# A two-layer trunk on one core: tap sums in PSUM, tap products and window adds on GpSimd, three units in split form

## The reference

```
h = rms_norm(x, norm_g)
proj = h @ w_in                      # 1024 -> 1024 (a) + 1024 (bv) + 1024 (bg) + 2048 (z)
pooled[g] = mean of a[g] over the last 2, 4, 8, 16 tokens - a[g]     # four groups of 256 channels
ya = (pooled[g] @ pool_w[g]) * pool_scale
u = bv * sigmoid(bg)
u = causal depthwise convolution of u, 31 taps, + conv_b             # 1024 channels
yb = silu(layer_norm(u))
x = x + (concat(ya, yb) * silu(z)) @ w_out
```

## Time and profile before

| | before |
|---|---|
| median of three runs | 333.19 us |
| profiled execution, its own time | 332.93 us |
| its span | 331.1 us |
| TensorE busy | 325.2 us (98%) |
| VectorE busy | 257.3 us (78%) |
| ScalarE busy | 230.5 us (70%) |
| GpSimd busy | 47.9 us (14%) |
| TensorE's granted clock | 0.998 |

### The profile page before, as it was taken

One profiled execution on the slowest core, in us unless ns is written; L12 is line 12 of the kernel. 1 busy time (PEld: TensorE's weight loads), 2 busy tenths in 40 slices (PEclk: granted clock), 3 DMA queues, 4 the chain that ended last, 5 costly groups with the idle time before them and its releaser, 6 DMA issues.

```text
span 331.1 us, 5733 instructions
## 1 busy us (share of the span) xinstructions
PE 325.2 (98%) x2196; PEld 296.1 (89%) x2196; DVE 257.3 (78%) x469; ACT 230.5 (70%) x439; POOL 47.9 (14%) x54
## 2 busy tenths in 40 slices
PE   8999999999999999999999999999999999999995
PEld 8899999999999999997999999988887776778885
DVE  2799999999989998987785898747556877748633
ACT  4687899997999697936775557824756666575630
POOL 0040022322322210120000000005500231400000
PEclk9999999999999999999999999999999999999999
DMA  7988039969979997676729343790635423200003
GB/s 276 409 318 322 2 100 356 242 167 334 266 195 315 175 423 227 129 183 198 256 99 420 117 138 135 275 344 8 247 127 167 135 97 128 113 0 2 0 2 127
DMA packets 12266, 62.67 MB, mean 189 GB/s; under 512 B 1360, under 2 KB 1488, under 8 KB 5968
## 3 DMA queue, kind: packets, MB, share of 16 engines
q1 hardware_dynamic: 8064, 53.78, 43.7%
q0 software_dynamic: 4032, 8.39, 14.1%
q10 hardware_dynamic: 144, 0.15, 0.2%
HBM read 52.88 MB, written 1.05 MB: 163 GB/s over the span
## 4 chain that ended last, share of the span: by engine, by line
PE 97%; DVE 1%; ACT 1%; issue 0%; POOL 0%; ACTq 0%; POOLq 0%
PE bank L1047 24%; PE bank L1048 23%; PE bank L1049 23%; PE bank L1081 8%; PE bank L1107 5%; PE bank L1155 2%; PE bank L1261 2%; PE bank L1288 2%; PE bank L1124 2%; PE bank L1274 2%; PE bank L1115 2%; PE bank L1240 1%; ACT scratch L458 1%; DVE scratch L741 1%; DVE scratch L854 0%
## 5 line engine op out<-in xcount | busy, mean ns | idle before, releaser
L712 DVE TENSOR_TENSOR w_lo<-raw,w_hi 128x1024 fp32r<-128x1024 f32 x78 | 92.6, 1220 | 16.9 <-ACT w_hi L450 16.8
L450 ACT CAST w_hi<-raw 128x1024 fp32r<-128x1024 f32 x82 | 82.2, 1047 | 3.5 <-PE bank L1049 3.5
L1047 PE MATMUL bank<-h_hi,w_hi 128*128 128x256 f32 x288 | 82.4, 286 | 0.0
L1049 PE MATMUL bank<-h_hi,w_lo 128*128 128x256 f32 x288 | 81.5, 283 | 0.0
L1048 PE MATMUL bank<-h_lo,w_hi 128*128 128x256 f32 x288 | 81.5, 283 | 0.0
L1048 PEld LDWEIGHTS bank<-h_lo,w_hi 128*128 128x128 f32 x288 | 55.3, 192 | 0.1
L1047 PEld LDWEIGHTS bank<-h_hi,w_hi 128*128 128x128 f32 x288 | 55.2, 192 | 0.1
L1049 PEld LDWEIGHTS bank<-h_hi,w_lo 128*128 128x128 f32 x288 | 55.2, 192 | 0.0
L1047 PE MATMUL bank<-w_hi,h_hi 128*128 128x512 f32 x96 | 39.2, 408 | 0.0
L533 ACT ACTIVATE scratch<-scratch,params 128x256 f32<-128x256 f32 x92 | 38.4, 504 | 0.0
L1047 PE MATMUL bank<-ya_hi,w_hi 128*128 128x256 f32 x128 | 38.1, 297 | 0.0
(11 more groups left out here) (106 smaller groups left out, 538.6 us busy)
## 6 DMA issues: line engine op xcount, KB each, us to landing
raw<-w SPq DMA_DIRECT2D x49, 1024.0 KB, 5.9
side_v<-side_ring POOLq DMA_DIRECT2D x24, 256.0 KB, 7.4
w_lo<-raw POOLq DMA_DIRECT2D x4, 512.0 KB, 5.6
X<-xT SPq DMA_DIRECT2D x2, 512.0 KB, 5.1
out<-X SPq DMA_DIRECT2D x4, 256.0 KB, 2.6
consts<-const SPq DMA_DIRECT2D x1, 290.0 KB, 13.4
params<-vec ACTq DMA_DIRECT2D x1, 149.0 KB, 4.8
```

Of the source, the lines that this page charges most:

```text
L450: nc.scalar.copy(halves(w_hi, cut_slot(n), half), halves(raw, n % RAW, half)).then_inc(hi_cut, 1)
L712: nc.vector.tensor_tensor(halves(w_lo, cut_slot(n), half), halves(raw, n % RAW, half), halves(w_hi, cut_slot(n), half).bitcast(F32), ALU.s ...
L1047: nc.tensor.matmul(dst, wh, ah, start=start, stop=False, skip_group_check=True)
L1049: return nc.tensor.matmul(dst, wl, ah, start=False, stop=stop, skip_group_check=True)
```

## The change

Four things change together, all in slots 2 to 21.

Units 5, 9 and 13 are taken out of `NATIVE`: they are now split, so that ScalarE and VectorE have three more units to cut, in slots 3, 7 and 11.

The running sums of the convolution start in PSUM banks 4 to 7 (`partial`), a tile's 256 columns each. Up to the start of slot 15 VectorE's taps read and write them there. In slot 15 four adds of two tiles bring each sum together with a second one in V and leave it in V (L918), from where all goes on as before. Unit 16 writes the same banks, so TensorE now waits before it for the last of these four (`tap` at `MERGED`).

GpSimd gets arithmetic. For every pair of tiles ScalarE writes one tap product into V (L650), and more of them into two buffers in turns; GpSimd adds 14 of these to V (L505, `pool_conv`), so 18 tap products of two tiles leave VectorE's list. A GpSimd add of slot n waits until VectorE has cut the low part of unit n + 2 (`pool_gate`); ScalarE's product for an add waits for the add two before it (`pool_tap`), since it writes the same buffer. GpSimd also makes the ten shifted adds of the pool mixer (L490); VectorE keeps the mean (L897 to L903), which now stands behind the taps of its slot, and for group 3 in slot 13.

The plan of taps is worked out anew with these costs. The ring of product buffers for VectorE's adds changes (`HOMES`, `FREE_AT`).

```diff
-NATIVE = frozenset((0, 5, 9, 13, 16, 21, 23, 25))
+NATIVE = frozenset((0, 16, 21, 23, 25))
...
+POOL_ADDS = {4: (0,), 5: (0, 0), 6: (0, 1), 7: (1, 1), 8: (1, 2), 13: (2, 3), 14: (2, 3, 3)}
+POOL_FIRST = (3, 5, 7, 9)
...
+def pool_gate(n):
+
+    return 2 * low_cuts(n + 2) + 2 if n + 2 not in NATIVE and n + 2 not in ADDED else 0
...
+            def pool_sums(g):
+
+                pool.wait_ge(a_ready, g + 1)
...
+                    nc.gpsimd.tensor_tensor(dst[:, :, lo:APAD + S], src[:, :, lo:APAD + S],
+                                            src[:, :, lo - shift:APAD + S - shift], ALU.add).then_inc(win, 1)
...
+            def pool_conv(n):
+
+                gate = pool_gate(n)
+                for pair, k, add, made, ready in POOL_PLAN[n - 1]:
+                    if add is None:
+                        continue
+                    if gate:
+                        pool.wait_ge(lo_cut, gate)
+                    if ready:
+                        pool.wait_ge(pool_tap, ready)
+                    pool.wait_ge(pool_product, made)
+                    nc.gpsimd.tensor_tensor(V[:, 2 * pair:2 * pair + 2, :], V[:, 2 * pair:2 * pair + 2, :],
+                                            pool_home(add), ALU.add).then_inc(pool_tap, 1)
...
+                if BG[1] < n <= MERGE_SLOT:
+                    side_sums(n - 1)
+                    if n - 1 in A:
+                        pool_sums(n - 1 - A[0])
+                if BG[1] < n <= MERGE_SLOT:
+                    pool_conv(n)
...
-                        nc.scalar.activation(V[:, c, :], U[:, c, 0:S], ACT.Identity, bias=column(CB + c),
+                        nc.scalar.activation(partial((c,)), U[:, c, 0:S], ACT.Identity, bias=column(CB + c),
...
+                for pair, k, add, made, _ in POOL_PLAN.get(n, ()):
+                    if add is None:
+                        act.wait_ge(u_ready, pair + 1)
+                    elif add >= 2:
+                        act.wait_ge(pool_tap, add - 1)
...
+                    total = partial(tiles) if done <= MERGED else V[:, c:c + 2, :] if len(tiles) == 2 else V[:, c, :]
+                    if k is None and product is None:
+                        dve.wait_ge(pool_tap, POOL_LAST[c // 2])
+                        dve.wait_ge(pool_product, POOL_MADE)
+                        nc.vector.tensor_tensor(V[:, c:c + 2, :], total, V[:, c:c + 2, :], ALU.add).then_inc(tap, 1)
...
-                if m in A:
-                    window_sums(m - A[0])
...
+                if n == A[3] + 2:
+                    window_sums(3)
                 taps(n)
+                if m in A[:3]:
+                    window_sums(m - A[0])
...
+                    pe.wait_ge(tap, MERGED)
```

More of the change, by code:

```diff
@@ L148, with pool_products @@
 SIDE_ITEMS = 14
-PRODUCTS = 4
-LATE_RING = 4
+EARLY_RING, MID_RING, LATE_RING = (0, 1, 2), (0, 1, 3), (4, 5, 6, 3)
 LATE_SLOT = A[3] + 3
+MERGE_SLOT = PW - 1
+POOL_ADDS = {4: (0,), 5: (0, 0), 6: (0, 1), 7: (1, 1), 8: (1, 2), 13: (2, 3), 14: (2, 3, 3)}
+POOL_FIRST = (3, 5, 7, 9)
+def pool_products():
+    plan, taken, count, made, last = {}, {pair: 0 for pair in range(4)}, 0, 0, {}
+    for n in range(BG[1], MERGE_SLOT):
+        plan[n] = []
+        firsts = (POOL_FIRST.index(n),) if n in POOL_FIRST else ()
+        for i, pair in enumerate(firsts + POOL_ADDS.get(n + 1, ())):
+            k = FIRST_POOL[pair] - taken[pair]
+            taken[pair] += 1
+            made += 1
+            first = i < len(firsts)
+            count += not first
+            plan[n].append((pair, k, None if first else count - 1, made, last.get(pair, 0)))
+            if not first:
+                last[pair] = count
+    return plan, taken, last
 def side_taps(pair):
     return range(TAPS - SIDE_ITEMS, TAPS) if pair < SIDE else ()
+FIRST_POOL = [TAPS - 1 - (SIDE_ITEMS if pair < SIDE else 0) for pair in range(4)]
+POOL_PLAN, POOL_TAKEN, POOL_LAST = pool_products()
+POOL_MADE = sum(POOL_TAKEN.values())
+def pool_gate(n):
+    return 2 * low_cuts(n + 2) + 2 if n + 2 not in NATIVE and n + 2 not in ADDED else 0
 def side_items(n):
     return [(pair, n - BG[pair + 1]) for pair in range(SIDE) if 0 <= n - BG[pair + 1] < SIDE_ITEMS]
-def product_free(product):
-    if product >= LATE_FROM:
-        return PRODUCT_USED[product - LATE_RING] if product - LATE_FROM >= LATE_RING else None
-    return PRODUCT_USED[product - PRODUCTS] if product >= PRODUCTS else 0
 def slot_work(n):
@@ L191, in conv_plan @@
 def conv_plan():
-    plan, last, used, count, before, late, folded = {}, {}, [], 0, None, None, []
-    left = {pair: [k for k in range(1, TAPS) if k not in side_taps(pair)] for pair in range(4)}
+    plan, last, used, count, before, late, folded, homes, free_at = {}, {}, [], 0, None, None, [], [], []
+    left = {pair: list(range(1, FIRST_POOL[pair] - POOL_TAKEN[pair] + 1)) for pair in range(4)}
     folds = [2 * pair + (SIDE_ITEMS + i) % 2 for pair in range(SIDE) for i in range(2)]
@@ L202, in conv_plan @@
         act_time = min(act_time, ACT_CARRY) + ACT_SHARE * length - act
+        for pair in range(4) if n == MERGE_SLOT else ():
+            tiles = CONV_PAIRS[pair]
+            count += 1
+            plan[n].append((tiles, None, None, max(last[c] for c in tiles), count))
+            dve_time -= 0.61
+            last.update({c: count for c in tiles})
+        if n == MERGE_SLOT:
+            merged = count
         while dve_time > 0 or n == OA[0]:
@@ L215, in conv_plan @@
                 used.append(count)
+                ring = EARLY_RING if n < A[3] + 1 else MID_RING if n < LATE_SLOT else LATE_RING
+                homes.append(ring[len(homes) % len(ring)])
+                free_at.append(max([u for u, h in zip(used[:-1], homes[:-1]) if h == homes[-1]], default=0))
                 dve_time, act_time = dve_time - 0.61, act_time - 0.8
@@ L230, in conv_plan @@
             last.update({c: count for c in tiles})
-    return plan, last, used, late, folded
+    return plan, last, used, late, folded, merged, homes, free_at
 DVE_SHARE, ACT_SHARE, NEW_LAST, ACT_CARRY = 0.95, 0.95, 40, 1.0
-CONV_PLAN, TILE_DONE, PRODUCT_USED, LATE_FROM, FOLDED = conv_plan()
+CONV_PLAN, TILE_DONE, PRODUCT_USED, LATE_FROM, FOLDED, MERGED, HOMES, FREE_AT = conv_plan()
 MEAN_AT = 1, 1, 7
@@ L416, in _, with side_sums @@
             pool.wait_ge(pads_set, 3)
-            for n in range(BG[1], OA[0]):
+            def side_sums(n):
                 for pair, item in side_items(n):
@@ L517, in _ @@
                 if n == ZA[0]:
-                    act.wait_ge(tap, PRODUCT_USED[LATE_FROM - 1])
+                    act.wait_ge(tap, max(MERGED, PRODUCT_USED[LATE_FROM - 1]))
                 if n - 1 in ZA:
@@ L529, in _ @@
                         act.wait_ge(pooled, 4)
-                    if product_free(product):
-                        act.wait_ge(tap, product_free(product))
+                    if FREE_AT[product]:
+                        act.wait_ge(tap, FREE_AT[product])
                     for i, c in enumerate(tiles):
@@ L551, in _ @@
                     side_product(pair, item)
+                for pair, k, add, made, _ in POOL_PLAN.get(n, ()):
[3 more added lines that the diff above has]
+                        act.wait_ge(pool_tap, add - 1)
+                    to = V[:, 2 * pair:2 * pair + 2, :] if add is None else pool_home(add)
+                    for i, c in enumerate(CONV_PAIRS[pair]):
+                        last = nc.scalar.mul(to[:, i, :], U[:, c, k:k + S], column(CW + TAPS * c + k))
+                    last.then_inc(pool_product, 1)
                 if n in A:
@@ L816, in taps @@
             def taps(n):
-                for tiles, k, product, ready, _ in CONV_PLAN.get(n, ()):
+                for tiles, k, product, ready, done in CONV_PLAN.get(n, ()):
                     c = tiles[0]
```

63 lines of the change are left out of this document (37 added, 26 removed).

## The result

The changed kernel takes 351.74 us (median of 4 runs, 351.67 to 351.82) against 333.22 for the kernel before, run beside it: 1.0556 times as long, interval 1.0543 to 1.0569, or 18.5 us more. Its span is 349.9 us against 331.1.

A forecast was written before the change was run, and what follows sets the result against it. The prediction took TensorE, busy 98% of the span, to bound the kernel before. It added 12.9 us of wait at unit 16 and 1.5 of cold start to 332.93, then 0.26 for the median: 347.6 us, range 342 to 354.

The forecast's parts named there:

- The path that the prediction bet on: Rings of waits between GpSimd, ScalarE and VectorE delay unit 16 by 12.9 us, plus slow clock 1.5: 347.6, chance 0.67.
- the rival of blocked cuts: In four groups GpSimd's window adds hold up one VectorE cut each, 4.8 us, giving 352.4; chance 0.15 shared with slow adds.
- TensorE's list and VectorE's own list: TensorE's work 3.4 us shorter, unit 16 at 102.9 if nobody is late; VectorE done at 99.0 if it never waits.
- No idle before unit 13: A sign to look for: TensorE hardly idle before unit 13, but idle some 10 to 16 us before unit 16.
- The ring of slots 5 to 7: GpSimd add, ScalarE product, high part and low part wait for each other; 7.0 us a turn against TensorE's 5.76.
- The ring of `pooled`: In slots 10 and 11, copy, high part, low part, taps and window rest wait in turn: 7.3 and 7.15 us.
- The chain of slots 12 to 14: From unit 14's high part through GpSimd's adds and ScalarE's late product to VectorE's four adds, done at 119.2.
- GpSimd's add: One 128 x 512 add takes 1.2 us (0.53 to 1.53); nine stand on the path, each 0.1 being 0.9 us.
- The cold start: After standing some 13 us ahead of unit 16, TensorE runs slowly at first: 1.5 us, from 0 to 2.2.
- cuts and adds in each other's way: The rival of blocked cuts again: VectorE's cuts and GpSimd's window adds exclude each other, 352.4; chance 0.15 with slow adds.
- adds of 2.0: GpSimd adds taking 2.0 us instead of 1.2 bring over 9 us, giving 357; chance 0.15 shared with blocked cuts.
- The other side: No wait at unit 16: the rings don't bind, unit 16 starts at 102.9, time 329.8 us; chance 0.04.

The follow-up runs named there:

- run 1: The changed kernel with units 5, 9 and 13 native again, the rest of the change kept: 350.86 us, ratio 1.0534.
- run 4: The changed kernel with 28 unread matmuls on TensorE ahead of its wait before unit 16: 349.85 us, ratio 1.0501.
- Run 10: The changed kernel with the four adds in slot 14, no GpSimd gate, mean ahead of taps, unit 9 native, five tap adds, new planner shares: 331.45 us, ratio 0.9950.
- run 3: The changed kernel with GpSimd's tap adds no longer waiting for VectorE's low cuts (`pool_gate` 0): 350.21 us, ratio 1.0511.
- run 8: The changed kernel with the four adds out of PSUM in slot 14 instead of 15, taps planned anew: 342.84 us, ratio 1.0298.

## Why the prediction came out right, and where it was off

The forecast of 347.6 with a range of 342 to 354 held the 351.74; slower by over 0.2% had 0.94. The mechanism was right, the size 4.1 us short. The path that the prediction bet on had 342.6 to 351 as its own ends, and 351.74 lies above them: the range held because its upper end took in the rival of blocked cuts. Point by point:

- *TensorE's list and VectorE's own list.* Right in kind. The 3.4 us of the split are hidden by the wait (run 1), and VectorE has room by its own work: it stands idle where the prediction said (1.65 before the cuts of slots 10 to 12, where 1.8 was said; 3.68 before L928 of slot 14, where about 5 was), and taps in PSUM go at 0.40 from start to start, as those in SBUF.
- *No idle before unit 13.* Not quite: of the small waits shown above 2.14 us stand right ahead of it.
- *The ring of slots 5 to 7.* The prediction has the low part of units 7, 8 and 9 done at 46.9, 53.9 and 60.8; in the trace it is done at 47.1, 54.2 and 61.1. The low part of unit 10 starts at 65.79 instead of 65.5. Up to here the path is right to 0.3 us.
- *The ring of `pooled`.* The ends of the window rest were put at 75.9, 83.2 and 90.3; they come at 77.4, 85.6 and 93.6. Here the step failed that gave a cut 2.3 us whatever GpSimd does. The cuts beside window adds take 3.81, 3.25, 3.29 and 3.29, together 4.2 us over four of 2.36. The three of them that stand ahead of 93.6 bring 3.3, the whole gap there; the fourth is not on the path.
- *The chain of slots 12 to 14.* First half of unit 15's high part at 98.8, product at 109.0, low part of unit 17 at 114.4, four adds at 119.2; found at about 102.2, 112.9, 118.2 and 122.9. The gap grows from 3.4 to 3.9: the two adds at 104.66, beside VectorE's two instructions of 30 columns, take 2.89 where 2.4 was counted, and ScalarE's product waits for what comes behind them. That the two small instructions themselves take over a microsecond each costs nothing, since VectorE waits there anyway.
- *GpSimd's add.* Taken at 1.2; the 14 tap adds take 1.40 in the mean. In slots 5 to 8 two adds take 2.5 to 2.7; the first window add of a group, over within 0.2 us of the start of the cut beside it, takes 1.08 (three of L490 in the changed kernel, of 540 columns). The estimate of 1.12 for 512 columns from the Trainium skill, "GPSIMD Engine Reference", section 3.1, agrees with it. Beside cuts the means are 1.8 to 1.9. The prediction called itself wrong if adds took over 1.6: for six of the ten window adds that is what happened (1.9 to 2.05 each).
- *The cold start.* Taken at 1.5, found at 2.05, and by itself 1.9 (run 4). The granted clock is 0.50 when unit 16 starts. The Trainium skill, "TensorE: Matmul & The Clock Gate", Part 1, has an idle TensorE fall to 1.2 GHz; the trace agrees.
- *The rival "cuts and adds in each other's way"* gave 352.4, by one add on each of four cuts, 4.8. It was the better figure, with 4.2 on the cuts, of which 3.3 on the path, and 351.74 in the end. The two do not exclude each other: it was a term of the sum rather than another case, and should have stood in it. Its other half, adds of 2.0, was put at over 9 us; by the prediction's own 0.9 us for each 0.1 it would be 7.2, and 354.8.
- *"No row excludes it."* The prediction says that VectorE and GpSimd are never both busy with arithmetic in the trace before. They are, late in it, and it shows. L435 on GpSimd (8 columns, one input) takes 0.24 five times and 0.81 to 1.16 three times, the 1159 ns of the earlier trace rows; each of these three overlaps half a cut and ends just after it. The first, VectorE and then GpSimd:

```profile
225.52 1.23 DVE L712 TENSOR_TENSOR w_lo<-raw,w_hi 128x1024 fp32r<-128x1024 f32 x1 [0.25 <-ACT w_hi L450]
```
```profile
226.03 0.81 POOL L435 TENSOR_SCALAR scratch<-scratch 128x8 f32<-128x8 f32 x1
```

  Here GpSimd is the one held up. So a row of before did speak for the rival.
- *The other side*, no wait at unit 16, needed all rings to be loose. Run 10 shows what that takes: an earlier fold, no gate, the mean ahead of the taps, one split less and nine adds less. Of these only two were tried alone, and neither does it: run 3 gives 1.5 us, run 8 gives 8.9.

The sum by terms is then: start of unit 16 at 123.06, of which 119.2 was forecast, 3.3 is from three cuts held up and some 0.5 from the adds of slot 13; 2.05 instead of 1.5 for the clock; 16.74 and 2.05 over the kernel before.

Not settled: how the two engines take turns. In run 3 a half of a cut (1.2 us alone) lasts 3.9 and 4.4 and so waits for two adds or more in a row, in the changed kernel for less than one; no run varied the order in which they meet. Nor did a run show a one-input instruction of this size on GpSimd with VectorE idle, so its own duration is open, and so is why it took longer than an add.

## What to carry to other kernels

Price a move to a helper engine by the ring that it closes, not by the work it takes away: follow one turn from row to row and compare it with what the bounding engine needs for a unit. Work on GpSimd with two SBUF inputs was in this kernel not beside VectorE's two-input work but in turns with it; keep it to where VectorE reads PSUM or waits, and let it be little. A fold that frees a resource for the bounding engine goes as early as its inputs allow, with nothing queued ahead of it that could come later.
